# Moving a weight panel's cast between activation tiles, and reordering the first step of the third feed-forward layer

## The chip, the cores and the metric

The kernel runs on one core of a Trainium2 chip. The metric is the device time of one execution in microseconds (us); smaller is better. The engines are named as in the profile: PE is TensorE (its matmuls), PEld its weight loads, ACT is ScalarE, DVE is VectorE, POOL is GpSimd, and SP is the engine that issues most DMAs.

## The reference

Two transformer blocks of width 1024 follow one another on 512 tokens, in float32. What matters here is the first layer and the last one:

```
first_block:  x = x + 0.5 * swiglu(rms_norm(x, ffn1_norm), w_gate, w_up, w_down)
              ...
second_block: h2 = rms(x, norm2_w) * (1 + sc2) + sh2
              up = h2 @ w_up                       # 1024 -> 2 * 2816
              up = causal depthwise conv of width 3 over the tokens (up) + conv_b
              val, gate = split(up)
              x = x + g2 * ((silu(gate) * val) @ w_down)
```

The program calls the three feed-forward layers ffn1, ffn2 and ffn3. Ffn3 is the one with the convolution. In ffn3 "gate" in the program's loops stands for the first panel of a step (the value half) and "up" for the second.

## The kernel before

**Precision.** Every float32 product is made of three products of a rounded type: activation high x weight high, activation low x weight high, activation high x weight low. So each weight panel (128 x 2048, 1 MB) that SP loads into `w_raw` is cast by ACT into `w_hi` (`split` on ACT, line 722), and DVE subtracts to get `w_lo` (`split` on DVE, line 1281). There are two buffers of each, used in turn: panel n+2 goes where panel n was. So ACT's cast of panel n+2 waits until PE has finished with panel n (`pe_done`), and SP's load of panel n waits until DVE has split panel n-2 (`w_split`). Activations are kept as `h_hi` and `h_lo`, eight tiles k of 128 features x 512 tokens.

**Order of the work.** Each engine has one program written out by hand; the engines meet on counting semaphores, and an engine does its instructions in order. Nothing is scheduled at run time.

**The start.** PE turns x (`L2362`), DVE copies each tile k out of PSUM (line 1588), ACT makes `h_hi` of tile k as x times a gain (`scaled_hi`, line 768), and DVE makes `h_lo` (line 1301). After its eight tiles ACT casts the first weight panel in two halves (lines 862 and 864); the first half releases PE (`w0_begun`) and the second its tile 4 (`w_hi_done`). PE then runs `first_gate` (line 2237): all eight tiles of h_hi with w_hi, all of h_lo with w_hi (both line 2250), then `first_sums` (line 2366) and last the products with w_lo (line 2255). `first_sums` turns parameter rows (2372, 2375) and adds the squares of x: its products at line 2378 wait, one block of tokens at a time, for ACT. ACT's program between the first panel and these is: cast of panel 1 (once it has landed), four squares of x (line 868), four scaled identities (line 870).

**Before ffn3.** `w_out2` ends with tile 7 of x, of which PE makes the two halves of the tokens (c = 0 and 1, 256 tokens each) one after the other. The norm "p2" of ffn3 is done by halves too. Its 16 items s are (k, c): s 0 to 7 are the eight tiles of the first half, 8 to 15 those of the second. DVE multiplies x by gain and root (`half_h`, line 1341) into a slot of `tmp`, ACT adds the shift and rounds to `h_hi` (`half_cast`, line 766), DVE makes `h_lo` from both (`half_lo`, line 1347). The root of half c needs the sum of squares of that half from PE (`half_sums`, lines 2193 to 2200), ACT's reciprocal root (line 759) and three DVE steps (1332 to 1334). `slot` (line 382) says which part of `tmp` an item uses; the squares of tiles 6 and 7 lie in `tmp` 2 and 3.

**Ffn3's first step** (`first_step`, line 2871) works on panels n (gate, banks 0 and 1) and n+1 (up, banks 2 and 3) by halves of the tokens. `gate(k, c)` is 6 products of 256 columns (with w_hi and w_lo, line 2882), `up(k, c)` is 4 (with w_hi alone, line 2894), `up_low(c)` is 16 with w_lo (line 2901), which need DVE's split of panel n+1. At the end of the gate's last product PE raises `pe_done`.

**The steps after it** are a loop: PE does 48 products of 512 columns of the gate, then 48 of the up (line 2232). Before the gate PE waits for two things:

```
pe.wait_ge(S("w_split"), i * 2 + (base + half + 1))
free(i, half)     # ffn3: pe.wait_ge(S("ffn3_conv"), i * 8 + (4 * half + 4))
```

The first is DVE's split of the step's panel; the second is the convolution of the step before, which reads banks 0 and 1. What ACT and DVE do between the last gate product of one step and the first of the next stands in their loops:

```
ACT: split(panel n+2)          waits for pe_done of panel n, then CAST (722)
     own tap of tiles 0, 1     out of banks 0, 1 (line 1251)
DVE: split(panel n+2)          waits for the CAST (line 1281)
     other taps of tiles 0, 1  four instructions out of banks 0, 1 (line 2119)
```

Of the kernel before, what the change touches and what calls it, by code (L numbers as in the profile page):

```python
# [37 lines left out]
KD = D // P  # L38
# [17 lines left out]
PANEL = 2048  # L56
# [76 lines left out]
def build(nc, inp, rel_onehot, out):  # L133
# [12 lines left out]
    with ExitStack() as ctx:  # L146
# [5 lines left out]
        def S(name):  # L152
            if name not in sems:
                sems[name] = ctx.enter_context(nc.semaphore(name))
            return sems[name]
# [15 lines left out]
        gain1 = sb("gain1", [P, 2 * KD])  # L171
# [10 lines left out]
        w_raw = [sb(f"w_raw{i}", [P, PANEL]) for i in range(2)]  # L182
        w_hi = [sb(f"w_hi{i}", [P, PANEL], F32R) for i in range(2)]
        w_lo = [sb(f"w_lo{i}", [P, PANEL], F32R) for i in range(2)]
        tmp = sb("tmp", [P, 6, T])
# [147 lines left out]
        HALF = [slice(c * T // 2, (c + 1) * T // 2) for c in range(2)]  # L333
# [47 lines left out]

        def slot(s):

            return tmp[:, 2 + (s // 2 + 2) % 4, HALF[s % 2]]

        def pair(i, r):

# [319 lines left out]
        def _(act):  # L707
            done = Steps(act, S("act_done"))

            def split(n, i=None):  # L710

                if i is None:
                    if n >= END:
                        return
                    i = n
                    act.wait_ge(S(f"w_landed{i % 2}"), 16 * (n // 2 + 1))
                    if n >= 2:
                        act.wait_ge(S("pe_done"), used(n - 2))
                else:
                    act.wait_ge(S(f"w_landed{i % 2}"), (n - (i % 2)) * 8 + 16)  # L720
                    act.wait_ge(S("pe_done"), (n - 2) * 4 + 4)
                act.copy(w_hi[i % 2][:], w_raw[i % 2][:]).then_inc(S("w_hi_done"), 1)  # L722
# [27 lines left out]
            def half_square(before, k, halves):  # L750

                wait_x(act, before, k, halves[-1])
                at = slice(HALF[halves[0]].start, HALF[halves[-1]].stop)
                act.activation(tmp[:, 2 + k % 2, at], x[:, k, at], ACT.Square).then_inc(S("norm_sq"), 1)

            def half_root(name, c):

                act.wait_ge(S("norm_summed"), NORM_SUM[name] + HALF_SUMS * (c + 1))
                act.activation(rstd[:, HALF[c]], half_sum(name, c), ACT.Abs_reciprocal_sqrt, scale=1.0 / D, bias=eps_col).then_inc(S("norm_root"), 1)

            def half_cast(name, shift, items):

                for s in items:
                    k, c = ITEMS[name][s]
                    act.wait_ge(S("norm_h"), NORM_H[name] + s + 1)
                    act.activation(h_hi[:, k, HALF[c]], slot(s), ACT.Identity, bias=shift(k)).then_inc(S("norm_hi"), 1)

            def scaled_hi(name, before, gain, ks):

                for k in ks:  # L770
                    wait_x(act, before, k)
                    act.activation(h_hi[:, k, :], x[:, k, :], ACT.Identity, scale=gain(k)).then_inc(S("norm_hi"), 1)
# [84 lines left out]
            act.wait_ge(S("cols_made"), 1)  # L857
            act.wait_ge(S("x_turned"), 1)
            act.activation(small[:, 0:KD], gain1[:, KD:2 * KD], ACT.Silu)
            scaled_hi("n1", "start", lambda k: gain1[:, k:k + 1], range(KD))  # L860
            act.wait_ge(S("w0_tables_landed"), 16)
            act.copy(w_hi[0][:, 0:PANEL // 2], w_raw[0][:, 0:PANEL // 2]).then_inc(S("w0_begun"), 1)
            act.wait_ge(S("w_landed0"), 16)
            act.copy(w_hi[0][:, PANEL // 2:], w_raw[0][:, PANEL // 2:]).then_inc(S("w_hi_done"), 1)
            split(1)
            for b in range(TB):
                squares = tmp[:, 2 * (b % 2):2 * (b % 2) + 2, :].rearrange("p k t -> p (k t)")
# [207 lines left out]
            n = PART["q2"][0]  # L1075
# [145 lines left out]
            n = PART["w_out2"][0]  # L1221
# [3 lines left out]
            shift2 = lambda k: mod[:, 24 + k:25 + k]  # L1225
# [1 line left out]
            half_square("mix2", 7, (0, ))  # L1227
            half_root("p2", 0)
            half_cast("p2", shift2, (0, 1))
            half_square("mix2", 7, (1, ))  # L1230
            half_cast("p2", shift2, (2, 3))
            half_root("p2", 1)
            n = BASE["ffn3"] + 1
            act.wait_ge(S(f"w_landed{n % 2}"), 16 * (n // 2 + 1))
            act.wait_ge(S("pe_done"), used(n - 2))
            for part in range(2):
                at = slice(part * PANEL // 2, (part + 1) * PANEL // 2)
                ins = act.copy(w_hi[n % 2][:, at], w_raw[n % 2][:, at])
                if part:
                    ins.then_inc(S("w_hi_done"), 1)  # L1240
                half_cast("p2", shift2, (4 + part, ))
            half_cast("p2", shift2, range(6, 2 * KD))
            base = BASE["ffn3"]
            with act.Fori(0, GU_STEPS) as i:
# [22 lines left out]
        def _(dve):  # L1267
# [59 lines left out]
            def half_root(name, c):  # L1327

                at = HALF[c]
                v, vr, r = tmp[:, 0, at], tmp[:, 1, at], rstd[:, at]  # L1330
                dve.wait_ge(S("norm_root"), NORM_ROOT[name] + c + 1)
                done(dve.scalar_tensor_tensor(v, half_sum(name, c), eps_width_col[D], r, ALU.add, ALU.mult))
                done(dve.scalar_tensor_tensor(vr, v, -0.5 / D, r, ALU.mult, ALU.mult))
                done(dve.scalar_tensor_tensor(r, vr, 1.5, r, ALU.add, ALU.mult))
# [383 lines left out]
            n = PART["v_gm"][0]  # L1718
# [10 lines left out]
            n, panels, _ = PART["u_gm"]  # L1729
# [152 lines left out]
            n, panels, _ = PART["b_proj"]  # L1882
# [15 lines left out]
            n, panels, _ = PART["w_out"]  # L1898
# [13 lines left out]
            for i, name in enumerate(("norm1_w_2", "norm2_w_2")):  # L1912
                at = 8 + 24 * i
# [53 lines left out]
            n = PART["q2"][0]  # L1967
# [3 lines left out]
            for b in range(TB):  # L1971
                dve.wait_ge(S("q2_out"), 2 * b + 2)
                ins = dve.tensor_reduce(stat[:, 8 * b:8 * b + 8], q_sq[:, b, :].rearrange("p (h d) -> p h d", d=QK), AX.X, ALU.add)
# [100 lines left out]
            n, panels, _ = PART["w_out2"]  # L2074
# [14 lines left out]
            p2 = lambda s: half_h("p2", lambda k: gain2[:, 1, k:k + 1], s)  # L2089
            p2_lo = lambda s: half_lo("p2", lambda k: mod[:, 24 + k:25 + k], s)  # L2090
# [8 lines left out]
            p2(3)  # L2099
            p2_lo(2)  # L2100
            p2_lo(3)
            half_root("p2", 1)
            for s in range(4, 2 * KD + 1):
                if s < 2 * KD:
                    p2(s)
                if s > 4:
                    p2_lo(s - 1)
                if s == 11:
                    split(BASE["ffn3"] + 1)
            base = BASE["ffn3"]  # L2110
            with dve.Fori(0, GU_STEPS) as i:
# [23 lines left out]
        def _(pe):  # L2135
# [439 lines left out]
            n = PART["b_proj"][0]  # L2575
# [11 lines left out]
            n = PART["q2"][0]  # L2587
# [283 lines left out]
            def first_step():  # L2871

                n = BASE["ffn3"]

                def gate(k, c):

                    wh, wl = panel(w_hi, n, KD, PC), panel(w_lo, n, KD, PC)
                    for low, terms in ((False, ((wh, h_hi), (wl, h_hi))), (True, ((wh, h_lo), ))):
                        ready_item("p2", k, c, low)
                        for t in range(2):  # L2880
                            for j, (w, h) in enumerate(terms):
                                mm = pe.matmul(B[t][:, HALF[c]], w[:, k, t * P:(t + 1) * P], h[:, k, HALF[c]],  # L2882
                                               start=k == 0 and not low and j == 0, stop=k == KD - 1 and low)
                            if (k, c, low) == (KD - 1, 1, True):
                                mm.then_inc(S("pe_done"), 2)

                def up(k, c):

                    wh = panel(w_hi, n + 1, KD, PC)
                    if (k, c) == (0, 0):  # L2890
                        pe.wait_ge(S("w_hi_done"), n + 2)
                    for t in range(2):
                        for h in (h_hi, h_lo):
                            pe.matmul(B[2 + t][:, HALF[c]], wh[:, k, t * P:(t + 1) * P], h[:, k, HALF[c]], start=k == 0 and h is h_hi, stop=False)  # L2894

                def up_low(c):

                    wl = panel(w_lo, n + 1, KD, PC)
                    for t in range(2):
                        for k in range(KD):  # L2900
                            mm = pe.matmul(B[2 + t][:, HALF[c]], wl[:, k, t * P:(t + 1) * P], h_hi[:, k, HALF[c]], start=False, stop=k == KD - 1)
                        if c:
                            mm.then_inc(S("pe_done"), 2)

                pe.wait_ge(S("w_split"), n + 1)
                for k in range(KD):
                    gate(k, 0)
                    if k == 1:
                        half_sums("p2", 1, (1, 3))
                    for u in {4: (0, 1, 2), 5: (3, ), 6: (4, ), 7: (5, 6, 7)}.get(k, ()):  # L2910
                        up(u, 0)
                for k in range(KD):
                    gate(k, 1)
                pe.wait_ge(S("w_split"), n + 2)
                up_low(0)
                for k in range(KD):
                    up(k, 1)
                up_low(1)

# [54 lines left out]
```

## Time and profile before

| | us |
|---|---|
| median of 3 runs | 1762.96 |
| lowest and highest run | 1761.33, 1763.87 |
| the profiled execution's own time | 1764.13 |
| its span, first to last instruction | 1761.4 |
| PE busy | 1742.2 (99%) |
| DVE, ACT, POOL busy | 1058.7, 741.0, 174.5 |

The span is what the trace covers; the time has 2.7 us more around it. With PE busy for 99% the other engines matter only where PE waits for one of them. The tables below give the start and length of instructions in us from the span's start. In a row that merges several instructions the length is their busy time together, and the bracket is the idle time of the engine just before them with what ended it. A PE product's length counts its drain too, which lies beside the next product, so the pace of PE is read from starts.

### The profile page before, as it was taken

To read this page: it belongs to the slowest core of one execution; us is meant where nothing else is said; L and a number is where in the kernel's file an instruction comes from. 1 tells how busy PE (TensorE), PEld (TensorE's weight loads), DVE (VectorE), ACT (ScalarE), POOL (GpSimd) and SP (SyncE) were. 2 spreads that over 40 slices of the span, in tenths; PEclk is the share of its full clock that TensorE was granted. 3 is DMA by queue.
4 is the path that set the end of the run, shared out by engine and by line. 5 is a ranking of instruction groups with operands and counts; after the bars stand their busy time and mean duration, and the time that the engine had idled before them with its cause. 6 is when DMAs were issued, how large, how long until landed. Compare 5 with 4: busy or idle time off the path is not lost.

```text
span 1761.4 us, 23716 instructions
## 1 busy us (share of the span) xinstructions
PE 1742.2 (99%) x8906; PEld 1425.8 (81%) x8906; DVE 1058.7 (60%) x1649; ACT 741.0 (42%) x1047; POOL 174.5 (10%) x229
## 2 busy tenths in 40 slices
PE   9999999999999999999999999999999999999998
PEld 7788888888888777788788888888987888888887
DVE  6666537555573667755789853447596665555433
ACT  5322222333444887623333322225575455555321
POOL 2222001120000000004411020120001200000000
PEclk9999999999999999999999999999999999999999
DMA  7777422343322211123655562325131223332232
GB/s 249 244 225 225 137 74 81 106 151 96 96 72 96 72 49 56 65 96 121 208 179 153 141 173 81 96 89 190 47 145 49 96 96 96 98 99 87 84 101 77
DMA packets 171714, 206.87 MB, mean 117 GB/s; under 512 B 18420, under 2 KB 150130, under 8 KB 171122
## 3 DMA queue, kind: packets, MB, share of 16 engines
q1 hardware_dynamic: 145010, 161.97, 28.7%
q0 software_dynamic: 12640, 38.55, 6.9%
q10 hardware_dynamic: 13984, 5.27, 1.4%
q8 instruction: 52, 0.85, 0.2%
q14 instruction: 28, 0.23, 0.0%
HBM read 190.29 MB, written 17.56 MB: 118 GB/s over the span
## 4 chain that ended last, share of the span: by engine, by line
PE 89%; DVE 5%; ACT 1%; DMA 1%; issue 1%; SPq 0%; DVEq 0%
PE bank L2232 39%; PE bank L2171 35%; PE bank L2507 5%; PE bank L2531 1%; PE bank L2628 1%; PE bank L2139 1%; DMA w_raw<-in_w_in 1%; PE bank L2541 1%; DVE w_lo L1281 1%; PE bank L2401 1%; PE bank L2882 1%; PE bank L2894 0%; PE bank L2250 0%; PE bank L2446 0%; PE bank L2190 0%
## 5 line engine op out<-in xcount | busy, mean ns | idle before, releaser
L722 ACT CAST w_hi<-w_raw 128x2048 fp32r<-128x2048 f32 x156 | 297.9, 1910 | 721.4 <-PE bank L2232 349.6
L1281 DVE TENSOR_TENSOR w_lo<-w_raw,w_hi 128x2048 fp32r<-128x2048 f32 x158 | 367.1, 2324 | 351.1 <-ACT w_hi L722 350.5
L2232 PE MATMUL bank<-h_hi,w_hi 128*128 128x512 f32 x1024 | 400.8, 391 | 1.7 <-DVE w_lo L1281 1.2
L2232 PE MATMUL bank<-h_hi,w_lo 128*128 128x512 f32 x1024 | 398.6, 389 | 0.0
L2232 PE MATMUL bank<-h_lo,w_hi 128*128 128x512 f32 x1024 | 315.4, 389 | 0.0
L2232 PEld LDWEIGHTS bank<-h_hi,w_hi 128*128 128x128 f32 x1024 | 192.2, 188 | 46.1 <-issue 4.3
L2232 PEld LDWEIGHTS bank<-h_lo,w_hi 128*128 128x128 f32 x1024 | 192.2, 188 | 40.2
L2232 PEld LDWEIGHTS bank<-h_hi,w_lo 128*128 128x128 f32 x1024 | 192.2, 188 | 39.2
L2171 PE MATMUL bank<-hid_hi,w_hi 128*128 128x512 f32 (+1 forms) x538 | 207.5, 386 | 0.0
L2171 PE MATMUL bank<-hid_lo,w_hi 128*128 128x512 f32 (+1 forms) x538 | 207.2, 385 | 0.0
L2171 PE MATMUL bank<-hid_hi,w_lo 128*128 128x512 f32 (+1 forms) x538 | 207.2, 385 | 0.0
L2171 PEld LDWEIGHTS bank<-hid_hi,w_hi 128*128 128x128 f32 x538 | 101.1, 188 | 20.5
L2171 PEld LDWEIGHTS bank<-hid_lo,w_hi 128*128 128x128 f32 x538 | 101.1, 188 | 20.1
L2171 PEld LDWEIGHTS bank<-hid_hi,w_lo 128*128 128x128 f32 x538 | 101.1, 188 | 20.1
L635 POOL TENSOR_TENSOR tmp<-x 128x512 f32<-128x512 f32 x24 | 37.2, 1548 | 729.9 <-DVE x L1902 307.4
L2171 PE MATMUL bank<-w_hi,h_hi 128*128 128x512 f32 (+1 forms) x240 | 91.2, 380 | 0.2 <-DVE w_lo L1281 0.2
L2171 PE MATMUL bank<-w_hi,h_lo 128*128 128x512 f32 (+1 forms) x240 | 90.1, 375 | 0.0
L2171 PE MATMUL bank<-w_lo,h_hi 128*128 128x512 f32 (+1 forms) x240 | 90.0, 375 | 0.0
L1475 DVE SCALAR_TENSOR_TENSOR mod_acc<-mod_raw,small,mod_acc 128x512 f32<-128x512 f32 x84 | 63.1, 751 | 23.7 <-DMA mod_raw<-in_w_mod 18.7
L1517 DVE TENSOR_TENSOR tmp<-tmp,bank 128x512 f32<-128x512 f32 x44 | 28.2, 682 | 74.1 <-PE bank L2232 74.1
L596 POOL DMA_DIRECT2D mod_raw<-in_w_mod x96 | 52.1, 544 | 189.6 <-DVE mod_acc L1472 129.6
L2119 DVE SCALAR_TENSOR_TENSOR tmp<-bank,vec,tmp 128x511 f32<-128x511 f32 x88 | 63.8, 745 | 6.4 <-DVE tmp L2119 1.7
(487 smaller groups left out, 2521.0 us busy)
## 6 DMA issues: line engine op xcount, KB each, us to landing
w_raw<-in_w_in SPq DMA_DIRECT2D x29, 1024.0 KB, 5.1
mod_raw<-in_w_mod POOLq DMA_DIRECT2D x96, 256.0 KB, 4.6
w_raw<-in_ffn_w_up SPq DMA_DIRECT2D x22, 1024.0 KB, 5.7
w_raw<-in_w_up SPq DMA_DIRECT2D x22, 1024.0 KB, 5.1
w_raw<-in_ffn_w_gate SPq DMA_DIRECT2D x21, 1024.0 KB, 5.5
w_raw<-in_ffn_w_down SPq DMA_DIRECT2D x16, 768.0 KB, 4.5
w_raw<-in_ffn_w_down SPq DMA_DIRECT2D x16, 640.0 KB, 4.0
w_raw<-in_w_out SPq DMA_DIRECT2D x8, 1024.0 KB, 5.2
```

Of the source, the lines that this page charges most:

```text
L596: pool.dma_start(mod_raw[:, k % MOD_SLOTS, :], wm[:, k, bass.ds(i * T + first * T, T)])\
L635: done(pool.tensor_tensor(tmp[:, min(k, 1), :], x[:, k, :], x[:, k, :], ALU.mult))
L722: act.copy(w_hi[i % 2][:], w_raw[i % 2][:]).then_inc(S("w_hi_done"), 1)
L1281: dve.tensor_tensor(w_lo[s][:], w_raw[s][:], w_hi[s][:].bitcast(F32), ALU.subtract).then_inc(S("w_split"), 1)
L1475: ins = dve.scalar_tensor_tensor(mod_acc[:], mod_raw[:, k % MOD_SLOTS, :], small[:, k:k + 1], mod_acc[:], ALU.mult, ALU.add)
L1517: dve.tensor_tensor(tmp[:, 2 + t, :], tmp[:, t, :], B[2 + t][:], ALU.mult).then_inc(S("hid"), 1)
L2119: dve.scalar_tensor_tensor(y[:, back:], up[:, :T - back], col_at(f"conv_w_2:{2 - back}", i * 2, KF * half + t), y[:, back:], ALU.mult, ALU ...
L2139: mm = pe.matmul(out_ap, stationary, moving, start=first and i == 0, stop=last and i == len(terms) - 1)
L2171: mm = pe.matmul(out_ap, stationary, moving, start=first and i == 0, stop=last and i == total - 1)
L2232: mm = pe.matmul(bank[:], w[:, k, at], h[:, k, :], start=k == first and part == 0 and i == 0, stop=k == last and part == 1)
L2401: mm = pe.matmul(bank(b)[:], own(h[:, k], b), w[:, k, :], start=k == 0 and wait is ready_hi and i == 0, stop=False)
L2507: mm = pe.matmul(beside_bank(name, t)[:], stationary, moving, start=j == 0, stop=j == 3 * k - 1)
```

## The change

There are three edits at the start, in the norm and in the first step of ffn3.

- At the start ACT casts the first half of the first panel after six tiles of h_hi instead of eight, the second half after the seventh; the eighth comes last.
- `slot` places items 4 to 7 otherwise in `tmp`, so that items 4 and 5 lie over squares of the first half, which are done with. ACT casts the first half of panel n+1 (up) right after items 0 and 1, the second half after items 2 and 3. DVE makes items 4 and 5, high and low, ahead of the second half's root. ACT's second root comes after its items 4 and 5. PE adds the second half's squares after the gate's tile 3 instead of tile 1. DVE splits panel n+1 after item 8 instead of item 11.
- In the second half of the tokens PE does `up_low(0)` first and then alternates gate(k, 1) and up(k, 1), where before all eight gate(k, 1) came first, then `up_low(0)`, then all eight up(k, 1).

```diff
--- before.py
+++ after.py
@@ -381,7 +381,7 @@
 
         def slot(s):
 
-            return tmp[:, 2 + (s // 2 + 2) % 4, HALF[s % 2]]
+            return tmp[:, 2 + s % 2, HALF[s // 2 % 2]] if s % 8 >= 4 else tmp[:, 4 + s // 2 % 2, HALF[s % 2]]
 
         def pair(i, r):
 
@@ -857,11 +857,14 @@
             act.wait_ge(S("cols_made"), 1)
             act.wait_ge(S("x_turned"), 1)
             act.activation(small[:, 0:KD], gain1[:, KD:2 * KD], ACT.Silu)
-            scaled_hi("n1", "start", lambda k: gain1[:, k:k + 1], range(KD))
+            gain_of = lambda k: gain1[:, k:k + 1]
+            scaled_hi("n1", "start", gain_of, range(6))
             act.wait_ge(S("w0_tables_landed"), 16)
             act.copy(w_hi[0][:, 0:PANEL // 2], w_raw[0][:, 0:PANEL // 2]).then_inc(S("w0_begun"), 1)
+            scaled_hi("n1", "start", gain_of, (6, ))
             act.wait_ge(S("w_landed0"), 16)
             act.copy(w_hi[0][:, PANEL // 2:], w_raw[0][:, PANEL // 2:]).then_inc(S("w_hi_done"), 1)
+            scaled_hi("n1", "start", gain_of, (7, ))
             split(1)
             for b in range(TB):
                 squares = tmp[:, 2 * (b % 2):2 * (b % 2) + 2, :].rearrange("p k t -> p (k t)")
@@ -1227,18 +1230,15 @@
             half_square("mix2", 7, (0, ))
             half_root("p2", 0)
             half_cast("p2", shift2, (0, 1))
-            half_square("mix2", 7, (1, ))
-            half_cast("p2", shift2, (2, 3))
-            half_root("p2", 1)
             n = BASE["ffn3"] + 1
             act.wait_ge(S(f"w_landed{n % 2}"), 16 * (n // 2 + 1))
             act.wait_ge(S("pe_done"), used(n - 2))
-            for part in range(2):
-                at = slice(part * PANEL // 2, (part + 1) * PANEL // 2)
-                ins = act.copy(w_hi[n % 2][:, at], w_raw[n % 2][:, at])
-                if part:
-                    ins.then_inc(S("w_hi_done"), 1)
-                half_cast("p2", shift2, (4 + part, ))
+            act.copy(w_hi[n % 2][:, 0:PANEL // 2], w_raw[n % 2][:, 0:PANEL // 2])
+            half_square("mix2", 7, (1, ))
+            half_cast("p2", shift2, (2, 3))
+            act.copy(w_hi[n % 2][:, PANEL // 2:], w_raw[n % 2][:, PANEL // 2:]).then_inc(S("w_hi_done"), 1)
+            half_cast("p2", shift2, (4, 5))
+            half_root("p2", 1)
             half_cast("p2", shift2, range(6, 2 * KD))
             base = BASE["ffn3"]
             with act.Fori(0, GU_STEPS) as i:
@@ -2099,13 +2099,17 @@
             p2(3)
             p2_lo(2)
             p2_lo(3)
+            p2(4)
+            p2(5)
+            p2_lo(4)
+            p2_lo(5)
             half_root("p2", 1)
-            for s in range(4, 2 * KD + 1):
+            for s in range(6, 2 * KD + 1):
                 if s < 2 * KD:
                     p2(s)
-                if s > 4:
+                if s > 6:
                     p2_lo(s - 1)
-                if s == 11:
+                if s == KD:
                     split(BASE["ffn3"] + 1)
             base = BASE["ffn3"]
             with dve.Fori(0, GU_STEPS) as i:
@@ -2905,15 +2909,14 @@
                 pe.wait_ge(S("w_split"), n + 1)
                 for k in range(KD):
                     gate(k, 0)
-                    if k == 1:
+                    if k == 3:
                         half_sums("p2", 1, (1, 3))
                     for u in {4: (0, 1, 2), 5: (3, ), 6: (4, ), 7: (5, 6, 7)}.get(k, ()):
                         up(u, 0)
-                for k in range(KD):
-                    gate(k, 1)
                 pe.wait_ge(S("w_split"), n + 2)
                 up_low(0)
                 for k in range(KD):
+                    gate(k, 1)
                     up(k, 1)
                 up_low(1)
```

## Rows read from the trace of the kernel before

**Rows 1.** The page's busy time of each engine, and its clock row in 40 slices.
```profile
PE 1742.2 (99%) x8906; PEld 1425.8 (81%) x8906; DVE 1058.7 (60%) x1649; ACT 741.0 (42%) x1047; POOL 174.5 (10%) x229
...
PEclk9999999999999999999999999999999999999999
```

**Rows 2.** Waits of the whole run: engine, line, what it waited for, total, times, longest.
```profile
PE bank L2882 <- ACT h_hi L766: 1.8, 2, 1.6
```

**Rows 3.** Timeline of PE, 0 to 25.
```profile
1.31 3.78 PE L2348 MATMUL bank<-ones 128*128 128x128 f32 x16 [1.31 <-POOL ones L584]
...
10.99 1.50 PE L2348 MATMUL bank<-ones 128*128 128x128 f32 x12
14.18 3.92 PE L2250 MATMUL bank<-h_hi,w_hi 128*128 128x512 f32 x16 [1.68 <-ACT w_hi L862]
...
23.14 1.34 PE L2378 MATMUL bank<-tmp,ones 128*128 128x128 f32 x8 [0.41 <-ACT tmp L870]
```

**Rows 4.** The chain that ended last, 1370 to 1420: start, length, engine, line.
```profile
1398.03 0.72 PE bank L2882 x6
...
1401.38 5.76 PE bank L2882 x48
...
1409.07 3.84 PE bank L2894 x32
```

**Rows 5.** Timeline of ACT, 6.5 to 25.5: start, length, instruction, count, idle before.
```profile
10.63 2.56 ACT L772 ACTIVATE h_hi<-x,gain 128x512 fp32r<-128x512 f32 x4 [0.50 <-DVE x L1588]
13.09 1.03 ACT L862 CAST w_hi<-w_raw 128x1024 fp32r<-128x1024 f32 x1
...
16.05 1.91 ACT L722 CAST w_hi<-w_raw 128x2048 fp32r<-128x2048 f32 x1 [0.97 <-DMA w_raw<-in_ffn_w_up]
...
22.59 1.28 ACT L870 ACTIVATE tmp<-ident,stat 128x128 f32<-128x128 f32 x4
```

**Rows 6.** Timeline of ACT, 23 to 66.
```profile
45.97 1.91 ACT L722 CAST w_hi<-w_raw 128x2048 fp32r<-128x2048 f32 x1 [12.08 <-DMA w_raw<-in_ffn_w_up]
```

**Rows 7.** Timeline of DVE, 20 to 62.
```profile
56.38 3.11 DVE L1475 SCALAR_TENSOR_TENSOR mod_acc<-mod_raw,small,mod_acc 128x512 f32<-128x512 f32 x4 [2.12 <-DMA mod_raw<-in_w_mod]
```

**Rows 8.** Timeline of ACT, 1378 to 1425.
```profile
1388.97 0.42 ACT L754 ACTIVATE tmp<-x 128x256 f32<-128x256 f32 x1 [0.54 <-DVE x L2086]
1389.76 0.91 ACT L766 ACTIVATE h_hi<-tmp,mod 128x256 fp32r<-128x256 f32 x2 [0.37 <-DVE tmp L1341]
...
1407.18 1.90 ACT L722 CAST w_hi<-w_raw 128x2048 fp32r<-128x2048 f32 x1 [0.41 <-PE bank L2882]
```

**Rows 9.** Timeline of PE, 1378 to 1425.
```profile
1389.72 0.59 PE L2197 MATMUL bank<-tmp,ones 128*128 128x256 f32 x2
...
1390.83 0.47 PE L2882 MATMUL bank<-h_hi,w_hi 128*128 128x256 f32 x1
...
1394.18 0.39 PE L2882 MATMUL bank<-h_hi,w_hi 128*128 128x256 f32 x1 [1.57 <-ACT h_hi L766]
```

**Rows 10.** Timeline of DVE, 1378 to 1425.
```profile
1390.30 0.89 DVE L1347 SCALAR_TENSOR_TENSOR h_lo<-tmp,mod,h_hi 128x256 fp32r<-128x256 f32 x2 [0.18 <-ACT h_hi L766]
1391.72 0.42 DVE L1332 SCALAR_TENSOR_TENSOR tmp<-bank,rstd 128x256 f32<-128x256 f32 x1 [0.54 <-ACT rstd L759]
...
1393.10 0.88 DVE L1341 SCALAR_TENSOR_TENSOR tmp<-x,gain,rstd 128x256 f32<-128x256 f32 x2
...
1399.88 2.28 DVE L1281 TENSOR_TENSOR w_lo<-w_raw,w_hi 128x2048 fp32r<-128x2048 f32 x1
...
1409.20 2.29 DVE L1281 TENSOR_TENSOR w_lo<-w_raw,w_hi 128x2048 fp32r<-128x2048 f32 x1 [3.22 <-ACT w_hi L722]
...
1412.31 2.30 DVE L2119 SCALAR_TENSOR_TENSOR tmp<-bank,vec,tmp 128x510 f32<-128x510 f32 x3 [0.15 <-DVE tmp L2119]
```

**Rows 11.** Timeline of PE, 1414 to 1416.
```profile
1414.66 0.50 PE L2232 MATMUL bank<-h_hi,w_hi 128*128 128x512 f32 x1
```

**Rows 12.** Waits of PE from 1414 to the end.
```profile
PE bank L2930 <- DVE x L1562: 0.4, 1, 0.4
```

## The prediction

> **What bounds the kernel now.** I began with the page's busy times and its clock row [rows 1]: PE is busy for 99% of the span at full granted clock. So the time is PE's own work plus its waits, and this change neither adds nor removes a product. All it can do is remove waits of PE or make new ones. The list of waits of the whole run names what may be removed near the edits: the first ffn3 step waits 1.8 us for `h_hi` in two pieces, 1.6 the longest [rows 2], and the first gate of ffn1 waits 1.68 us for the first half of the panel's cast (the bracket at 14.18) [rows 3]. I then read ACT, PE and DVE in order of time around both places, and looked for who takes over when PE arrives earlier. The chain that ended last served for the pace of the ffn3 step [rows 4].
>
> **Part 1, the start.** ACT's eight `h_hi` end with the cast's start at 13.09 [rows 5]; the last four come every 0.62 us ((13.09 - 10.63) / 4). With six tiles ahead the cast begins at 13.09 - 2 x 0.62 = 11.85, so PE may begin its gate 1.24 us earlier, at about 12.95 instead of 14.18. What PE needs next is there in time: tile 7 of `h_hi` ends near 15.2, since ACT's work is only reordered, and PE comes to it seven tiles of 2 x 0.23 us after its start, at 16.2. The sum of ACT's work up to panel 1 is unchanged, and ACT then waits for the landing of panel 1 at 16.05 anyway, with 0.97 us of idle ahead of it [rows 5]; that idle is the cover for the second half's later end.
>
> From 16.05 nothing of ACT moves: cast, four squares, four identities from 22.59 to 23.87 [rows 5]. PE's squares' products start at 23.14, having waited for these identities (0.41 us) [rows 3], and four identities 0.32 us apart pace them to their end. So PE arrives 1.2 us earlier and waits 1.2 us longer: the gain is nothing. Were this wait not there, two more would hold it back: ACT has panel 3 only at 45.97, after 12.08 us of waiting for its DMA [rows 6], and DVE waits for a modulation load until 56.38 [rows 7], behind which stands the split of the second step after. Moved DMAs: none at the start, since SP's and POOL's loads wait for DVE's splits and DVE's split of panel 0 still follows the eight low tiles; POOL's clearing of `zero` may come some tenths earlier. Bounds: -1.2 us if the early start were all kept, 0 on the other side because of the 0.97 us of idle. I take 0, the value of the two nearest rows (22.59 and 23.14).
>
> **Part 2, first half of the tokens in ffn3.** Until 1389.7 nothing moves. The cast's first half (1.04 us) goes into the gap of ACT between items 0, 1 and the square at 1388.97 [rows 8]: it runs 1388.4 to 1389.4, and the square follows to 1389.8. Its panel has long landed. Items 2 and 3 then start at 1389.8, as now (1389.76). PE now does the second half's squares at 1389.72, and goes on with gate(2, 0) from 1390.83, in effect 1.3 us later, since that product is longer than those behind it [rows 9]. In the changed order it goes to gate(2, 0) at once, and item 2 is there at 1390.3: a new wait of 0.6 us. Two gates at 0.72 us [rows 4] end at 1391.75, the squares at 1393.05. Gate(4, 0) then starts at once: its item 4 is made by DVE after the low items of 1390.30 [rows 10], so from 1391.2, by ACT after the cast's second half by 1392.2, and low by 1392.7. So it starts at 1393.1 instead of 1394.18 [rows 9]: **-1.1 us**. The root follows the squares, as now: PE's 1389.72, DVE's root 2.0 us later at 1391.72, item 4 another 1.38 later at 1393.10 [rows 9, 10]. In the changed kernel squares at 1391.75 give the root at 1393.75 and item 6 from 1395.1, cast by 1396.2, low by 1396.7. PE comes to gate(6, 0) near 1396.7, so that is just covered; here is 0.1 to 0.3 us of risk. DVE's split of panel n+1 starts after item 8, near 1397.4, instead of 1399.88, and ends at 1399.7 [rows 10]; PE is through the first half at 1401.4 - 1.1 = 1400.3 and needs it then, for `up_low(0)`. Covered by 0.6 us. SP's load of panel n+3 waits for this split and so starts 2.4 us earlier, with nothing beside it. Bounds: gain of 0.3 (item 6 late) to 1.6 (the whole old wait).
>
> **Part 3, second half of the tokens.** PE's products are the same, and DVE's two instructions of an item take 0.9 us (0.88 / 2 and 0.89 / 2 [rows 10]) where PE takes 1.20 us for a pair (0.72, and four products of 3.84 / 32 = 0.12 [rows 4]), so inside the stretch nothing waits. But the end of the gate moves. Now the eight gates run first, and the last ends at 1401.38 + 5.76 = 1407.14 [rows 4]. Only then does PE release the panel's buffer and banks 0 and 1. ACT starts the cast of the next gate panel at 1407.18 [rows 8], DVE its split at 1409.20, then the four taps, of which the last ends at 1412.31 + 2.30 = 1414.61 [rows 10]. The next step's gate waits for both, and starts at 1414.66 [rows 11]. PE meanwhile had `up_low(0)` (16 x 0.12 = 1.92), eight ups (3.84) and `up_low(1)` (1.92), 7.7 us: a cover that fits the 7.5 us of this chain with next to nothing over.
>
> In the changed order the gate ends at 1400.3 + 1.92 (`up_low(0)`) + 7 x 1.20 + 0.72 = 1411.3. Behind it PE has one up (0.48) and `up_low(1)` (1.92): it is out of work at 1413.7. The cast, the split and the taps cannot begin before 1411.3: the cast overwrites the buffer that the gate reads, and the taps read its banks. They take 7.5 us as now (both engines are otherwise idle, as now), so the next gate starts at 1411.3 + 7.5 = 1418.8. PE stands still for 5.1 us, and step 1 starts 1418.8 - 1414.7 = **4.1 us** later than now. Two small checks on what is queued behind: ACT's cast of the next up panel and DVE's split of it come about 2 us later than now but have step 1's gate (48 products of 0.23 us, 11 us) as cover; SP's load behind the late split has a whole step. From 1414 to the end PE's only wait is 0.4 us [rows 12], so no slack takes the 4.1 us back. Bounds: 3.6 (no first-half risk, a chain of 7.3) to 4.9 (first half gains only 0.3).
>
> **The sum.** 0 + 4.1 (in which the 1.1 of the first half is counted). The profiled execution took 1764.13, 1.2 above the median of the three runs, so its own sum would be 1768.2; against the median 1762.96 it is **1767.1**.
>
> **A rule weighed.** The page of the profile has PE's clock at full level throughout [rows 1], and a pause of 1.68 us before the first gate is followed by 16 products in 3.92 us, the full pace [rows 3]. No row shows a pause of 5 us within the work. The Trainium skill ("TensorE: Matmul & The Clock Gate", section "HAM oscillation — how this bites in real kernels") says that too long an idle gap between bursts of matmuls makes the gate throttle the array again. No run here shows that yet; by the rule the sum would be larger by the price below.
>
> **The rivals.**
> - *The pause costs clock as well.* After 5.1 us without a product the clock falls from 2.4 to 1.2 GHz and the first products of step 1 run at half pace. The nearest rows: at the start, after nothing, 16 products take 3.78 us (0.236 each) where the same product later takes 1.50 / 12 = 0.125 [rows 3], so 16 x 0.111 = 1.8 us were lost, and more behind them. Price 1.8 to 3, taken as 2.4: 1769.5. For: the pause is three times the longest now. Against: no row shows a fall. Chance 0.33.
> - *The early start is kept after all.* If the identities were not what paces PE at 23.14 and nothing at 45.97 and 56.38 held it, 1.2 us would stay: 4.1 - 1.2 = 2.9, so 1765.9. Against: three rows say otherwise. With a shorter chain (7 us) it would come to the same. Chance 0.14.
> - *Not slower: the chain behind the gate is hidden.* Its place is the wait ahead of step 1's gate. If the chain were under 7.5 - 4.1 = 3.4 us, step 1 would start no later than now; at 2.4 us or less the first half's 1.1 us would be all gained: 1761.9. That needs the split done out of another buffer or the taps not waited for; the code has neither, and the cast and split alone take 1.90 + 2.29 [rows 8, 10]. Chance 0.05.
> - *The first half is late too* (item 6 or the split of panel n+1): up to 0.8 us more, 1767.9; in the forecast's range.
>
> **How the numbers follow.** The forecast with its bounds has 0.48. About 0.2%, 3.5 us, is what a measurement of this kernel can tell from no change. The forecast's 4.1 lies only 0.6 above it, so a quarter of its chance falls within 0.2%: 0.12; the kept start adds 0.11 and the hidden chain 0.01, which makes 0.24 same. Faster: 0.04. Slower: 0.72. Range: the kept start and somewhat below, to the clock rival with its upper price: 1764.3 to 1770.5. The likeliest case alone is 1766.4 to 1768.1.
>
> **What would show it.** In the changed profile: PE starts its first gate near 12.95 and has about 1.2 us more of waiting before line 2378, whose start stays at 23.1. In ffn3's first step a wait of some 0.6 us before gate(2, 0), none of 1.57 before gate(4, 0); `up_low(0)` 1.1 us earlier; then the last gate product ending near 1411.3, the taps near 1418.8, and a wait of PE for line 2119 or the split of about 5 us, which stands in no list now. If the clock row or the length of line 2232's first products after it shows half pace, the first rival holds. Wrong altogether: no such wait, with the gate's `pe_done` still ahead of the ups.

## The result, and the profile after

The changed kernel takes 1770.56 us (median of 6 runs, 1769.04 to 1771.92) against 1763.56 us before (6 runs). The ratio is 1.0044, 95% interval [1.0034, 1.0053]: 7.0 us slower, where 4.1 were forecast in a range up to 1770.5. In a later batch the same program was 6.3 us above before, 1.0034 [1.0021, 1.0047]. Two executions of that batch, one of the kernel before (8028 us) and one of the kernel with `up_low(0)` first (3536 us), are far off and are left out of the ratios. The profiled execution took 1771.92 us with a span of 1770.2.

The page, beside [rows 1]: the busy time of PE has risen by 2.9 us, with the same 8906 products. The clock row in tenths does not show why.

```profile
PE 1745.1 (99%) x8906; PEld 1427.9 (81%) x8906; DVE 1059.0 (60%) x1649; ACT 740.9 (42%) x1047; POOL 174.2 (10%) x229
...
PEclk9999999999999999999999999999999999999999
```

The list of PE's waits, beside [rows 2, 3] (engine, line, what it waited for, total, times, longest). Lines 722, 766, 1281 and 1347 stand as before; 862 is now 863, 870 is 873, DVE's 2119 is 2123, and lines of PE's program are 4 further on, so 2236 is the old 2232.

```profile
PE bank L2236 <- DVE tmp L2123: 5.1, 1, 5.1
PE bank L2236 <- DVE w_lo L1281: 3.2, 3, 1.7
...
PE bank L2382 <- ACT tmp L873: 1.0, 1, 1.0
PE bank L2254 <- ACT w_hi L863: 0.9, 1, 0.9
...
PE bank L2886 <- ACT h_hi L766: 0.7, 2, 0.4
```

What is new is one wait of 5.1 us before the gate of ffn3's step 1, for the taps of the convolution. The old wait of 1.6 us inside the first step has become two short ones, 0.7 together. At the start the wait for the cast has shrunk from 1.68 to 0.9, and the one for ACT's identities grew from 0.41 to 1.0. Both moved the way that was forecast, but by 0.8 and 0.6 us in this execution where the forecast had 1.2; the two timelines of the start, ACT's (beside [rows 5]) and PE's (beside [rows 3]):

```profile
12.85 1.03 ACT L863 CAST w_hi<-w_raw 128x1024 fp32r<-128x1024 f32 x1
...
16.45 1.92 ACT L722 CAST w_hi<-w_raw 128x2048 fp32r<-128x2048 f32 x1 [0.38 <-DMA w_raw<-in_ffn_w_up]
...
22.98 1.28 ACT L873 ACTIVATE tmp<-ident,stat 128x128 f32<-128x128 f32 x4
```

```profile
13.93 3.94 PE L2254 MATMUL bank<-h_hi,w_hi 128*128 128x512 f32 x16 [0.91 <-ACT w_hi L863]
...
23.53 1.33 PE L2382 MATMUL bank<-tmp,ones 128*128 128x128 f32 x8 [1.02 <-ACT tmp L873]
```

In this execution x arrived later: DVE's four last copies of x began at 10.89 instead of 9.91, so ACT cast at 12.85 and not at 11.85. PE's gate begins at 13.93, only 0.25 earlier than before, and the products of line 2382 (the old 2378) at 23.53, 0.39 later, behind identities at 22.98. So they gained nothing here. A cleaner case is the profile of a kernel below (the changed one with the old second half), which has the same start's edit and in which x came no later than before: its first gate begins at 12.62, 1.56 earlier than before, and its products of line 2382 at 23.14, to 0.01 us as before:

```profile
23.14 1.34 PE L2382 MATMUL bank<-tmp,ones 128*128 128x128 f32 x8 [1.97 <-ACT tmp L873]
```

Ffn3's first step on PE, ACT and DVE, beside [rows 9, 8, 10, 11]:

```profile
1392.97 0.38 PE L2886 MATMUL bank<-h_hi,w_hi 128*128 128x256 f32 x1 [0.43 <-ACT h_hi L766]
...
1395.65 0.47 PE L2886 MATMUL bank<-h_hi,w_hi 128*128 128x256 f32 x1
...
1402.54 2.17 PE L2905 MATMUL bank<-h_hi,w_lo 128*128 128x256 f32 x16
...
1414.14 2.08 PE L2905 MATMUL bank<-h_hi,w_lo 128*128 128x256 f32 x16
1421.34 0.79 PE L2236 MATMUL bank<-h_hi,w_hi 128*128 128x512 f32 x1 [5.12 <-DVE tmp L2123]
1421.93 0.63 PE L2236 MATMUL bank<-h_hi,w_lo 128*128 128x512 f32 x1
...
1425.77 0.69 PE L2236 MATMUL bank<-h_lo,w_hi 128*128 128x512 f32 x2
...
1426.54 0.40 PE L2236 MATMUL bank<-h_hi,w_lo 128*128 128x512 f32 x1
```

```profile
1413.86 1.90 ACT L722 CAST w_hi<-w_raw 128x2048 fp32r<-128x2048 f32 x1 [4.39 <-PE bank L2886]
```

```profile
1386.04 0.48 DVE L2086 SCALAR_TENSOR_TENSOR x<-bank,mod,x 128x256 f32<-128x256 f32 x1 [2.12 <-PE bank L2175]
...
1415.88 2.29 DVE L1281 TENSOR_TENSOR w_lo<-w_raw,w_hi 128x2048 fp32r<-128x2048 f32 x1 [7.20 <-ACT w_hi L722]
...
1418.99 2.30 DVE L2123 SCALAR_TENSOR_TENSOR tmp<-bank,vec,tmp 128x510 f32<-128x510 f32 x3 [0.15 <-DVE tmp L2123]
```

Executions differ in when they get here. In thirteen of the fourteen profiles of this document the addition to the first half of tile 7 begins between 1381.87 and 1383.81; in this one it begins at 1386.04. So I count from that addition, at 1386.04 here and at 1383.39 before. From there `up_low(0)` (line 2905) begins at 16.50 us; before, the second half of the tokens began at 1401.22, at 17.83. The first half gained 1.3 us. The cast that waits for the gate's end begins at 27.82, before at 23.79; the taps end at 1418.99 + 2.30; step 1 starts at **35.30, before at 31.27: 4.03 us later**. The forecast said 4.1.

The rest is in the last PE rows. From 1421.34 the products of 512 columns come 0.43 us apart, and from 1426.3 at 0.23 us as always. The windows around it (us, busy of PE, PEld, DVE, ACT, POOL with counts, granted clock, DMA share, GB/s):

```profile
1413.00:1419.00 6.00, 3.22 (x27) 3.02 (x26) 2.96 (x3) 5.14 (x5) 0.00 (x0) 1.00 0.00 1
1419.00:1424.00 5.00, 2.66 (x6) 2.15 (x7) 4.86 (x5) 2.53 (x3) 0.00 (x0) 0.51 0.66 213
1424.00:1430.00 6.00, 6.00 (x24) 4.79 (x23) 4.98 (x8) 3.66 (x5) 0.00 (x0) 0.84 0.55 175
```

The granted clock is full until 1419, falls to half (1.2 GHz) while PE stands still, and comes back only near 1426. From step 1's start to the first product of the down projection it takes 1641.38 - 1421.34 = 220.04 us; before, 1632.58 - 1414.66 = 217.92 (chain of waits). The clock's price is **2.1 us**. In the profile of the second batch it is 2.15, in that of the ffn3 edits alone 2.75. So 4.0 + 2.1 to 2.8 makes 6.1 to 6.8 us, beside 6.3 and 7.0 measured (and 5.5 for the ffn3 edits alone). The other 2.65 us by which this profiled execution is late lie before 1386 and are no part of the change's price: in the second batch's profile of the same program the addition begins at 1383.16, and the median is still 6.3 us above before.

### The profile page after: what moved, and what is told of

It reads as the page before. It is cut to its first block, busy times and chain, and to the rows that moved or that the text cites. A ratio compares the mean times of both kernels' runs of the same rounds, so it can differ in the third digit from the quotient of the medians.

```text
span 1770.2 us, 23716 instructions
## 1 busy us (share of the span) xinstructions
PE 1745.1 (99%) x8906; PEld 1427.9 (81%) x8906; DVE 1059.0 (60%) x1649; ACT 740.9 (42%) x1047; POOL 174.2 (10%) x229
## 4 chain that ended last, share of the span: by engine, by line
PE 89%; DVE 5%; ACT 1%; DMA 1%; issue 1%; SPq 0%; DVEq 0%; ACTq 0%
PE bank L2236 39%; PE bank L2175 35%; PE bank L2511 5%; PE bank L2535 1%; PE bank L2632 1%; DMA w_raw<-in_w_in 1%; PE bank L2143 1%; PE bank L2545 1%; DVE w_lo L1281 1%; PE bank L2405 1%; PE bank L2886 1%; PE bank L2254 0%; PE bank L2898 0%; PE bank L2450 0%; PE bank L2194 0%
```

## The experiments

Each kernel was timed in turn with the kernel before. In every case I give the median, the difference to before's median in the same batch, the ratio's interval, and "step 1": the time from DVE's addition to tile 7's first half until step 1's first product in the profile, 31.27 before. "Steps" is the time from there to the down projection, 217.92 before, which shows the clock.

**The two places apart.** First the start's edit alone:

```diff
-            scaled_hi("n1", "start", gain_of, range(KD))
+            gain_of = lambda k: gain1[:, k:k + 1]
+            scaled_hi("n1", "start", gain_of, range(6))
...
+            scaled_hi("n1", "start", gain_of, (6, ))
...
+            scaled_hi("n1", "start", gain_of, (7, ))
```

(The cast's two halves stand where lines are left out.)

> The kernel before with the start's edit alone. My theory: the earlier first gate is lost at the wait for ACT's identities, so the ratio to before is 1.000 (0 us, within 0.5), and the late DMA of panel 3 in the changed kernel's profile (47.92 against 45.97) is scatter between executions. Rival A, the start is kept: 1.2 us faster. Rival B, the start's edit itself makes panel 3 late: 0.5 to 2.4 us slower, with the cast of panel 3 near 47.9 again.

1763.34 us, +0.1, [0.9991, 1.0009]; step 1 at 31.28. Panel 3's cast at 45.17. In its list of waits PE waits 0.6 us for the cast instead of 1.7, and 0.6 for the identities instead of 0.4; it still waits 0.9 for the split at 62.40. The edit is worth nothing that can be measured and costs nothing. The late panel 3 of the changed kernel's profile (47.92) was scatter: over all profiles without the load swap its cast began between 41.31 and 47.92, with the start's edit (45.17, 41.31, 43.29, 45.78, 45.42, 47.92) as without (45.97, 44.66, 43.71, 43.43, 45.78).

Then the ffn3 edits alone (the whole diff but for the hunk at the start):

> The kernel before with the ffn3 edits alone. My theory: the whole loss of the change, 4.1 us of late gate end plus 2.4 us of lower clock, so about 6.5 to 7 us slower than before. Rival B (the start's edit costs up to 2.4 us): 4.5 to 6 us slower.

1768.73 us, +5.5, [1.0020, 1.0042]; step 1 at 35.29, steps 220.67. The whole loss is here. And the changed kernel again, unaltered:

> The changed kernel itself, unaltered, beside the other kernels of this batch. My theory: 4.0 us for the late gate end and 2.1 to 2.8 us for the lower clock, and nothing from the start, so 6 to 7 us above before; its start will show panel 3's cast anywhere between 41 and 48. Rival (the start's edit adds 2 us because panel 3 lands late): 8 to 9 us above, panel 3's cast again near 48.

1769.20 us, +6.3, [1.0021, 1.0047]; step 1 at 35.31, steps 220.07, panel 3 at 45.78. The step's numbers repeat to 0.02 us, so the profile can price a part of this step where the medians, with some 1 us of scatter, can't.

**Is it the pause that costs clock?** The pause was filled:

```diff
             first_step()
+            idle_products(20, ones[:], 5)
             gate_up("ffn3", ...)
```

> The changed kernel with 20 idle products of 128 columns, results unused, put behind the first ffn3 step, where PE otherwise waits 5.1 us. If the pause sends the clock down: the clock stays at full level, the first products of the next step come at 0.23 us instead of 0.43, and the time is 2.4 us below the changed kernel's, 4 to 5 us above before. If the slow products have another cause than the pause: no gain, 7 us above before.

1766.41 us, +3.2, [1.0007, 1.0025]; step 1 at 35.30, steps 217.87. Its first two products of step 1:

```profile
1417.64 0.50 PE L2236 MATMUL bank<-h_hi,w_hi 128*128 128x512 f32 x1 [0.65 <-DVE tmp L2123]
1417.98 0.39 PE L2236 MATMUL bank<-h_hi,w_lo 128*128 128x512 f32 x1
```

Step 1 starts as late as in the changed kernel, to 0.01 us, but at full pace (0.34 to the second product, 0.23 from then on). The clock's part is gone and only the late gate end is left; 4.0 lies in the interval (1.2 to 4.4 us), though the median itself shows 3.2. So the pause is what costs clock: the same 512-column products at the same place, with the same DMAs beside them, run at full pace once the pause is filled. The mean granted clock of its runs is 0.9994, of the changed kernel's in the second batch 0.9970, of the kernel before 0.9989 in the first batch and 0.9993 in the second.

With half the idle products (10, which the trace shows as 20 records):

> The changed kernel with 10 idle products behind the first ffn3 step instead of 20, so that a pause of about 2.6 us is left of 5.1. A pause of 1.8 us kept full clock and one of 3.7 us lost it. If what counts is the pause that is left: full clock, 4.0 us above before. If the idle products do not count as work: the clock falls as in the changed kernel, 6 to 7 us above before.

1767.91 us, +4.9, [1.0018, 1.0043]; step 1 at 35.31, steps 219.49.

```profile
1413.07 2.39 PE L2352 MATMUL bank<-ones 128*128 128x128 f32 x20
1418.35 0.50 PE L2236 MATMUL bank<-h_hi,w_hi 128*128 128x512 f32 x1 [2.89 <-DVE tmp L2123]
...
1419.22 0.63 PE L2236 MATMUL bank<-h_hi,w_lo 128*128 128x512 f32 x1
...
1423.02 0.39 PE L2236 MATMUL bank<-h_hi,w_lo 128*128 128x512 f32 x1
```

My reading "full clock" fell: after idle products up to 1415.5 and a wait of 2.9 us (I had reckoned 2.6), the first two products come at full pace, and from 1419.2 to 1422.8 they come at half. It costs 1.6 us. The fall came here *after* work had resumed. The other reading expected 6 to 7 us; the profile's 4.04 + 1.57 = 5.6 lies between the two, so how far idle products count as work stays open.

**How far the gate's end decides.** Two kernels with the changed first half and other orders of the second, without the start's edit. In the one, all eight ups stand in a loop of their own behind the gates. In the other, four of them stand beside their gates; its edit to the changed kernel (the start's, taken back, is left out):

```diff
                 for k in range(KD):
                     gate(k, 1)
+                    if k < 4:
+                        up(k, 1)
+                for k in range(4, KD):
                     up(k, 1)
                 up_low(1)
```

> The kernel before with the changed first half of ffn3's first step, and of the second half only up_low(0) moved ahead of the eight gates; then eight ups and up_low(1). The gate ends 1.9 us later than in the old order and the pause should be 5.12 - 7 x 0.48 = 1.8 us. My theory: step 1 starts 31.7 us after DVE's first half of tile 7, against 31.3 before, so 0.4 us slower than before, at full clock. Rival (any pause there costs clock): 2.5 us or more above before, with slow first products.

1763.70 us, +0.8, [0.9998, 1.0016]; step 1 at 31.94, steps 217.89.

```profile
1414.19 0.50 PE L2233 MATMUL bank<-h_hi,w_hi 128*128 128x512 f32 x1 [1.76 <-DVE tmp L2120]
1414.52 0.40 PE L2233 MATMUL bank<-h_hi,w_lo 128*128 128x512 f32 x1
```

> As the kernel with up_low(0) first, but the first four gates of the second half alternate with their ups. The gate ends 1.9 us later again, the pause should be 3.7 us, and step 1 starts 2.3 us later than before. If the clock falls in a pause of this length too: 4.4 to 5.1 us above before; if only longer ones count: 2.3 us.

1767.79 us, +4.8, [1.0013, 1.0034]; step 1 at 33.85, steps 220.58.

```profile
1415.79 0.79 PE L2233 MATMUL bank<-h_hi,w_hi 128*128 128x512 f32 x1 [3.68 <-DVE tmp L2120]
1416.38 0.63 PE L2233 MATMUL bank<-h_hi,w_lo 128*128 128x512 f32 x1
...
1421.75 0.40 PE L2233 MATMUL bank<-h_hi,w_hi 128*128 128x512 f32 x1
```

The gate's end moves by 1.9 us from one to the other (four ups of 0.48), and step 1 with it: 31.94, 33.85. From there to the changed kernel's 35.30 it is 1.45 us, three ups more. The pauses are 1.76, 3.68 and 5.12 us. The first is what moving `up_low(0)` (1.92) ahead of the gates took from the cover; to it the second adds four ups and the third three more. This is the mechanism of the forecast, in three sizes. The clock was lost after the two longer ones, at about the same price (2.66 and 2.1 to 2.75), and not after the short one.

**Does the first half's gain stay, with the old second half?** The changed kernel with the old order of the second half:

> The changed kernel with the second half of the tokens in its old order (eight gates, up_low(0), eight ups, up_low(1)); start and first half stay changed. My theory: no pause, step 1 starts about 1.1 us earlier than before, so 1.1 us faster than before. Rival (the loss is in the first half or the start): slower than before by over 1 us.

1763.15 us, -0.1, [0.9990, 1.0008]; step 1 at 30.93, 0.34 earlier than before, not 1.1. DVE and PE at the seam (its line 2886 is the gate's):

```profile
1396.35 2.28 DVE L1281 TENSOR_TENSOR w_lo<-w_raw,w_hi 128x2048 fp32r<-128x2048 f32 x1
...
1398.94 0.48 DVE L1347 SCALAR_TENSOR_TENSOR h_lo<-tmp,mod,h_hi 128x256 fp32r<-128x256 f32 x1
```

```profile
1399.48 0.50 PE L2886 MATMUL bank<-h_lo,w_hi 128*128 128x256 f32 x2
```

DVE splits panel n+1 after item 8's first instruction, so the low part of item 8 is done only at 1399.4, and gate(0, 1) waits for it. In the changed order `up_low(0)` stood there and hid this. The low products of the eight gates then start at 1399.48 to 1405.05, 0.80 us apart where PE's own work is 0.72: DVE, set back by the split, paces them with its two instructions an item. The first wait (0.3) and this pace (0.5) are most of the 1.0 us that went missing. So I gave the split to POOL, which is idle:

```diff
             norm("p2", "mix2")
+            n = BASE["ffn3"] + 1
+            pool.wait_ge(S("w_hi_done"), n + 1)
+            pool.wait_ge(S("w_split"), n)
+            pool.tensor_tensor(w_lo[n % 2][:], w_raw[n % 2][:], w_hi[n % 2][:].bitcast(F32), ALU.subtract).then_inc(S("w_split"), 1)
...
-                if s == KD:
-                    split(BASE["ffn3"] + 1)
```

> The kernel before with the changed first half, the old order of the second half, and the split of panel n+1 made by POOL instead of DVE. The kernel with the old second half kept only 0.3 us of the first half's 1.3 us, since DVE's split after item 8 makes item 8's low part late for gate(0, 1). If that is the reason: step 1 starts 1.3 us earlier after DVE's first half of tile 7 (29.9 to 30.1 us against 31.3) and the time is 1.3 us below before. Rival (POOL's split of 2048 columns takes over 8 us or slows DVE down): no gain or slower than before.

1765.44 us, +2.5, [1.0005, 1.0023]; step 1 at 34.58. A miss, by the rival's second half:

```profile
1391.78 4.67 POOL L708 TENSOR_TENSOR w_lo<-w_raw,w_hi 128x2048 fp32r<-128x2048 f32 x1 [11.18 <-ACT w_hi L1240]
```

```profile
1392.25 4.87 DVE L1348 SCALAR_TENSOR_TENSOR h_lo<-tmp,mod,h_hi 128x256 fp32r<-128x256 f32 x2 [0.18 <-ACT h_hi L770]
1397.05 0.41 DVE L1333 SCALAR_TENSOR_TENSOR tmp<-bank,rstd 128x256 f32<-128x256 f32 x1
```

POOL does the split in 4.67 us, fast enough. But DVE's two instructions for the low parts of items 4 and 5, 0.9 us together for other items in the same trace, take 4.87 us, 4.48 of them the first, which ends 0.3 us after POOL's. PE then waits 2.87 us for that low part, in the midst of the first half of the tokens, and the clock falls there too (windows as above, the granted clock 1.00 and then 0.50):

```profile
1394.00:1397.00 3.00, 0.22 (x1) 0.22 (x2) 3.00 (x2) 0.00 (x0) 2.44 (x1) 1.00 0.00 0
1397.00:1400.00 3.00, 3.00 (x16) 3.00 (x16) 2.71 (x8) 0.91 (x2) 0.00 (x0) 0.50 0.74 245
```

The products of 256 columns behind it come 0.21 us apart instead of 0.12 until 1400.4. So the late step 1 is this wait and some 1.6 us of lower clock, less the gain of the first half. The Trainium skill ("SBUF — State Buffer", section "Who interferes with whom") says that a DVE instruction with two inputs in SBUF and a GpSimd instruction that reads SBUF get in each other's way. These two are of that kind, and the 4.87 us agree with it.

**A version below before.** Panel 3 is loaded behind some 11 us of small loads on SP. The swap:

```diff
                     load(2, gate_v[:, :, PC:2 * PC], KD, PC)
+                    load(3, up_v[:, :, PC:2 * PC], KD, PC)
                     load_spread()
-                    load(3, up_v[:, :, PC:2 * PC], KD, PC)
```

> The kernel before with one swap on SP: panel 3's load is issued ahead of the small loads of load_spread instead of behind them. In the kernel before it is issued at 30.84 and cast at 45.97, and PE waits up to 1.2 to 3.2 us for splits behind it between 50 and 65. My theory: the cast of panel 3 comes before 40 and these waits go, 1 to 2 us faster than before. Rival (modulation loads or the later small loads take their place): 0.

1763.24 us, +0.3, [0.9992, 1.0010]; step 1 at 31.28. Panel 3's cast is at 40.88, and no split is waited for near 50 or 60, as expected. The room was small, though: in the profile before, PE waits for such a split only once, 1.2 us at 63.02 (the 3.2 us of the expectation is the changed kernel's sum). Nothing is gained in the median, where 1 to 2 us were expected. In this profile the first gate waited 2.5 us for the cast, since x came late; the clock fell behind it, and the products of line 2378 began at 25.08 instead of 23.14 (windows as above):

```profile
12.00:15.00 3.00, 0.55 (x6) 0.35 (x4) 3.00 (x5) 3.00 (x6) 0.00 (x0) 1.00 1.02 321
15.00:18.00 3.00, 3.00 (x10) 2.34 (x11) 3.00 (x6) 2.92 (x3) 1.79 (x3) 0.69 0.37 78
18.00:21.00 3.00, 3.00 (x11) 2.42 (x10) 2.90 (x2) 2.94 (x5) 0.57 (x2) 0.74 0.88 299
```

> The same swap together with the start's edit. My theory: the early first gate is lost at the wait for ACT's identities near 23, which the swap does not touch, so the time equals that of the swap alone within 0.5 us. Rival (the start's gain is real and was only lost at the late panel 3): 1.2 us below the swap alone.

1763.83 us, +0.8, [0.9995, 1.0014]: not below the swap alone, so the start's edit shows no gain with panel 3 early either; PE waits 2.0 us for the identities. In its profile the clock fell in ffn3's first step, over the old waits around 1390 to 1394, and step 1 came at 32.76:

```profile
1389.00:1392.00 3.00, 2.09 (x16) 1.80 (x14) 2.36 (x7) 1.56 (x3) 0.00 (x0) 1.00 0.00 0
1392.00:1395.00 3.00, 2.33 (x14) 2.21 (x15) 2.35 (x7) 2.34 (x5) 0.00 (x0) 0.86 0.00 0
1395.00:1398.00 3.00, 3.00 (x18) 3.00 (x17) 3.00 (x9) 1.95 (x4) 0.00 (x0) 0.57 0.00 0
```

The last kernel joins the swap, the start's edit and the first half, with the old second half and DVE's split behind item 15 (`if s == 2 * KD`):

> The swap, the start's edit and the changed first half of ffn3's first step, with the old order of the second half and DVE's split of panel n+1 moved to the end, behind item 15. My theory: gate(k, 1) no longer waits for low parts, up_low(0) waits about 0.5 us for the split, and step 1 starts 30.5 us after DVE's first half of tile 7 against 31.3 before: 0.8 us below the swap alone, 2 to 3 us below before.

1761.69 us, -1.3, [0.9983, 1.0001]; step 1 at 30.47, as expected (30.5). The split there starts right behind the last low part, and `up_low(0)` waits 0.3 us for it:

```profile
1403.78 2.28 DVE L1281 TENSOR_TENSOR w_lo<-w_raw,w_hi 128x2048 fp32r<-128x2048 f32 x1
```

Measured from before in each batch it is 7.6 to 8.3 us faster than the changed kernel, but its interval against before still touches 1: below before by 0.8 us in the step, and not shown to be so in the time. My 2 to 3 us counted on 1 to 2 from the load swap, which that kernel alone (+0.3) does not show.

## Why the prediction was right and wrong

- **Direction and mechanism: right.** Part 3's claim, that the gate's end rather than PE's own work sets step 1, is shown by the three orders of the second half. The forecast put the gate's end at 1411.3, the pause at 5.1 us, and step 1 4.1 us later. In the profile, less the 2.65 us by which everything is late, the cast starts at 1411.2, the pause is 5.12 us and the delay 4.03.
- **Part 2: right in kind, low in size.** A gain of 1.1 us was forecast for the first half, 1.3 was measured. The new wait before gate(2, 0) was 0.43 us, not 0.6, and the split of panel n+1 ended at 1402.47 for a product at 1402.54, with no 0.6 us to spare. That the gain would have been lost by gate(0, 1) in the old order I did not see, since the change has another order there.
- **Part 1: right.** The start alone gives 1.000. The wait for the identities takes it over, also when panel 3 is early; with x no later than before it is 1.97 us where 0.41 + 1.24 was forecast, and the products behind it start at 23.14 in both.
- **What failed is the sum's silence on the clock.** The sum's step from "PE stands still for 5.1 us" to "4.1 us later" took the pause as idle time alone; the price of the clock stood in it as nothing and was left to a rival with a chance of 0.33, because no row showed a fall. The fall came in every profile with a pause of 2.9 us or more in this place, five of five, and once more behind a wait of 2.87 us in the kernel with POOL's split. It was worth 2.1 to 2.75 us after pauses of 3.7 and 5.1 us and 1.6 us after the half-filled one; the rival said 1.8 to 3, taken as 2.4. Its sum was 6.5 us; the two differences measured are 6.3 and 7.0. So the mechanism was named and priced, and its chance was what was mis-sized. Of the 3.5 us between 1767.1 and the measured 1770.56, 2.1 to 2.75 are the clock and 0.6 is the kernel before: the forecast stood on a median of three, 1762.96, and the six have 1763.56. The range ended at 1770.5, which is 1762.96 + 4.1 + 3 and 0.4 us for scatter. The measured 1770.56 lies outside by 0.06 and the second batch's 1769.20 inside, so which side it fell on was chance; that the clock was missing from the sum was not. By the rule of the Trainium skill ("TensorE: Matmul & The Clock Gate", section "HAM oscillation — how this bites in real kernels") a long enough gap throttles the array; the trace agrees with 0.43 us in place of 0.23 per product after 5.12 us.
- **"Not slower" and "kept start"** are refuted: no profile with a late gate end had step 1 earlier, and the start's edit alone is within its interval of 1.000 ([0.9991, 1.0009]).

## What to carry to other kernels

When PE's products are reordered, ask for each group when its last one ends and what chain starts there; here a cast, a split and four taps, 7.5 us, began at the gate's last product, and the work that PE had behind it was almost exactly their cover. A new pause of PE is to be priced twice, once as idle time and once as slow products after it. Here the second price came in every profile with a wait of 2.87 us or more in ffn3, though the profile of before showed none. To keep the gain of an earlier first part, look also at what the next part's first item waits for on the engine that was made busier.

## What the runs showed of the hardware

- The clock fell after or in waits of PE of 2.9, 3.7 and 5.1 us in ffn3 (six profiles of six), and it kept full level after 1.76 us there (one profile). Elsewhere it also fell around smaller ones in single profiles (2.5 us at the start with the load swap; 1.6 us between short bursts in ffn3's old first step, with the swap and the start's edit). The kernel before and the one with the swap alone kept full clock at the same waits of ffn3, so these two falls are not foretold by the wait's length. Of the kernel before, in the third batch, the 8 runs with a mean clock of 1.000 took 1762.4 us on average and the 5 with 0.998 took 1763.7; in the first batch it was 1763.2 (7 runs) and 1764.0 (11). So small falls of the clock seem to be a part of the scatter; that was not tested by itself.
- The low level lasted past the pause: until nearly 5 us after work resumed in the changed kernel, and in the half-filled one it began 0.9 us after.
- While POOL's subtraction of 128 x 2048 ran (4.67 us), DVE's two instructions took 4.87 us in place of 0.9. So here POOL was no spare engine, although it was idle. Whether it is the operand form or any POOL work was not tried.
